# Differential attention on one core: the second map scaled by GpSimd alone, and three of four transposed copies on ScalarE

## What is computed

```python
sc = jnp.einsum('bqhmd,bkhmd->bmhqk', qb, k).astype(jnp.float32) * scale + bias[None, None]
p = jax.nn.softmax(sc, axis=-1)
a = p[:, 0] - lam * p[:, 1]
return jnp.einsum('bhqk,bkhd->bqhd', a.astype(v.dtype), v)
```

## Time and profile before

| what | value |
|---|---|
| median of 3 runs | 4088.17 us (4086.8 to 4090.68) |
| profiled execution, its own time | 4092.34 us |
| profiled execution, its span | 4090.5 us |
| TensorE busy | 3788.4 us (93%) |
| VectorE busy | 2234.5 us (55%) |
| ScalarE busy | 1657.8 us (41%) |
| GpSimd busy | 2488.2 us (61%) |
| differential stage, first maximum to last output | 1177.5 to 1697 us, and once more in the second layer |

### The profile page before, as it was taken

How to read it: one execution, slowest core, us unless ns; L and a number is a source line. 1 busy time by engine, 2 the same in 40 slices (tenths; PEclk the granted TensorE clock), 3 DMA queues, 4 the chain that set the end, 5 groups by cost and what they waited for, 6 DMA issues and landing times. The chain is left out here.

```text
span 4090.5 us, 51527 instructions
## 1 busy us (share of the span) xinstructions
PE 3788.4 (93%) x19002; PEld 2626.4 (64%) x19002; DVE 2234.5 (55%) x3991; ACT 1657.8 (41%) x2882; POOL 2488.2 (61%) x1393
## 2 busy tenths in 40 slices
PE   8999999999989899789889999999999898997898
PEld 8788774555546565558787897755555465655587
DVE  3012135555569999675430021255555699996754
ACT  3112104333358888661031121033333588886610
POOL 1221326877769999755512213277777699997555
PEclk9999999999989999999989999999999899999999
DMA  5333534342220222325353335323322202223353
GB/s 178 124 138 117 169 115 109 78 101 64 57 56 1 56 56 52 91 83 184 130 177 124 129 120 152 130 57 75 75 65 57 56 1 56 56 52 90 88 181 129
DMA packets 179680, 391.38 MB, mean 96 GB/s; under 512 B 17854, under 2 KB 98984, under 8 KB 167784
## 3 DMA queue, kind: packets, MB, share of 16 engines
q1 hardware_dynamic: 178568, 386.70, 33.9%
q10 hardware_dynamic: 864, 1.41, 0.2%
HBM read 254.88 MB, written 135.67 MB: 95 GB/s over the span
## 5 line engine op out<-in xcount | busy, mean ns | idle before, releaser
L1279 POOL TENSOR_TENSOR mla_sum_pool<-mla_sum_pool,mla_probs 128x1024 f32<-128x1024 f32 (+1 forms) x336 | 777.9, 2315 | 207.0 <-ACT mla_probs L1240 182.2
L1297 DVE TENSOR_REDUCE carry_row_max<-psum 128x1 f32<-128x512 f32 x688 | 474.4, 690 | 413.6 <-PE psum L1112 409.1
L1240 ACT ACTIVATE mla_probs<-psum 128x1024 f32<-128x1024 f32 x384 | 373.3, 1021 | 693.6 <-PE psum L1149 686.4
L1545 ACT ACTIVATE diff_probs<-psum,diff_shift 128x1024 f32<-128x1024 f32 x512 | 566.1, 1111 | 195.3 <-DVE diff_shift L1620 189.7
L1613 DVE TENSOR_REDUCE diff_row_max<-psum 128x1 f32<-128x1024 f32 x512 | 612.5, 1218 | 52.5 <-PE psum L1480 38.3
L1492 PE MATMUL psum<-ident,diff_probs 128*128 128x128 f32 x2048 | 329.8, 284 | 107.1 <-DVE diff_turned L1647 72.6
L624 PE MATMUL psum<-in_x_hi,in_w_hi 128*128 128x512 f32 x1024 | 404.5, 395 | 2.7 <-ACT in_mla_val L733 2.7
L624 PE MATMUL psum<-carry_firsts,in_w_hi 128*128 128x512 f32 x1024 | 404.8, 395 | 0.0
L624 PE MATMUL psum<-in_x_hi,in_w_lo 128*128 128x512 f32 x1024 | 401.6, 392 | 0.0
L1492 PEld LDWEIGHTS psum<-ident,diff_probs 128*128 128x128 f32 x2048 | 215.8, 141 | 285.5 <-issue 188.5
L1162 PE MATMUL psum<-mla_probs,mla_v_op 128*64 128x512 f32 x1536 | 373.1, 607 | 0.0
(11 more groups left out here) (206 smaller groups left out, 7369.1 us busy)
## 6 DMA issues: line engine op xcount, KB each, us to landing
in_w_raw<-in_w_in SPq DMA_DIRECT2D x64, 512.0 KB, 3.9
split_d<-in_out SPq DMA_DIRECT2D x64, 512.0 KB, 2.6
raw_d<-in_out SPq DMA_DIRECT2D x32, 512.0 KB, 2.6
mq_d<-in_out SPq DMA_DIRECT2D x48, 256.0 KB, 3.4
mk_d<-in_out SPq DMA_DIRECT2D x48, 256.0 KB, 3.8
carry_firsts<-split_d SPq DMA_DIRECT2D x48, 256.0 KB, 7.9
carry_weights<-split_d SPq DMA_DIRECT2D x48, 256.0 KB, 7.7
carry_weights<-split_d SPq DMA_DIRECT2D x16, 768.0 KB, 17.7
```

The source lines that it names most:

```text
L1240: nc.scalar.activation(probs[:, s % RING, :].rearrange("p (a n) -> p a n", n=CH), psum[:, S0 + 2 * (s % 2):S0 + 2 * (s % 2) + 2, :], ACT.E ...
L1279: nc.gpsimd.tensor_tensor(acc, start, probs[:, s % RING, mine], ALU.add).then_inc(pool_added, 1)
L1297: nc.vector.tensor_reduce(row_max[:, u % 2, qb, n:n + 1], psum[:, sweep_bank(g), :], AX.X, ALU.max).then_inc(maxed, 1)
L1545: nc.scalar.activation(dst[:, half * HALF:(half + 1) * HALF].rearrange("p (a n) -> p a n", n=CH), banks(n, m, half), ACT.Exp, bias=shift[: ...
```

## The change

GpSimd now scales all of `probs1` itself, with a tensor_scalar whose factor is the per-partition number, 1024 keys at a time, each followed by its add. ScalarE no longer scales (L1552 is gone). C0 moves from VectorE to ScalarE, where it stands behind C3 and ahead of E00. On TensorE S01 moves ahead of T3, directly behind S00. The scaling in the windowed attention becomes a tensor_scalar as well.

```diff
@@ tensor program @@
                     if on:
                         scores(n, 0, 0)
+                        scores(n, 0, 1)
                     turns(n - LAG - 1, 3)
-                    if on:
-                        scores(n, 0, 1)
                     products(n, 0)
                     turns(n - LAG, 0)
...
@@ scalar program @@
-                def scale(n):
-                    act.wait_ge(ratio_ready, n + 1)
-                    first = probs1[:, n % DEEP1, 0:CH]
-                    nc.scalar.activation(first, first, ACT.Copy, scale=ratio[:, n % 2:n % 2 + 1]).then_inc(act_scaled, 1)
...
                     copy(n - LAG - 1, 3)
+                    copy(n - LAG, 0)
                     if on:
                         exp(n, 0)
                     copy(n - LAG, 1)
-                    if 1 <= n <= UNITS:
-                        scale(n - 1)
...
@@ gpsimd program @@
-                    second, third = probs1[:, n % DEEP1, CH:HALF], probs1[:, n % DEEP1, HALF:SEQ]
-                    nc.gpsimd.tensor_tensor(second, second, ratio[:, n % 2:n % 2 + 1].broadcast_to([P, HALF - CH]),
-                                            ALU.mult).then_inc(times_ratio, 1)
-                    pool.wait_ge(act_scaled, n + 1)
...
+                    for half in range(2):
+                        at = slice(half * HALF, (half + 1) * HALF)
+                        nc.gpsimd.tensor_scalar(probs1[:, n % DEEP1, at], probs1[:, n % DEEP1, at],
+                                                ratio[:, n % 2:n % 2 + 1], None, ALU.mult).then_inc(times_ratio, 1)
+                        pool.wait_ge(times_ratio, 2 * n + half + 1)
+                        nc.gpsimd.tensor_tensor(probs[:, n % DEEP, at], probs[:, n % DEEP, at],
+                                                probs1[:, n % DEEP1, at], ALU.add).then_inc(mixed, 1)
...
@@ vector program @@
                         to_shift(n, 0)
-                    copy(n - LAG, 0)
                     ratios(n - 1)
...
@@ windowed attention, gpsimd program @@
-                        nc.gpsimd.tensor_tensor(row, row, inv[:, qb % 2, h:h + 1].broadcast_to([P, w]), ALU.mult
+                        nc.gpsimd.tensor_scalar(row, row, inv[:, qb % 2, h:h + 1], None, ALU.mult
                                                 ).then_inc(scaled, 1)
```

More of the change, by code:

```diff
@@ L1405, in diff_attention @@
             sem(n) for n in ("scored", "maxed", "shifted", "exped", "summed", "inverted", "ratio_ready"))
-        act_scaled, times_ratio, mixed, turn_done, copied, pv_done, odd_out, o_ready = (
-            sem(n) for n in ("act_scaled", "times_ratio", "mixed", "turn_done", "copied", "pv_done", "odd_out", "o_ready"))
+        times_ratio, mixed, turn_done, copied, pv_done, odd_out, o_ready = (
+            sem(n) for n in ("times_ratio", "mixed", "turn_done", "copied", "pv_done", "odd_out", "o_ready"))
         def banks(n, m, half):
```

## The result

The changed kernel takes 4439.49 us (median of 4 runs) against 4089.43 us for the kernel before, 1.0853 of its time with a 95% interval of 1.0837 to 1.087. That is 350 us more. I had forecast slower, but with 4161 us and an upper end of 4205: the direction was right and the size was far off.

The account below looks back on a forecast made before the run. GpSimd bounded the kernel at 7.83 us a unit; afterwards a ring through the early C0 would, at 8.47. +78 us for units and -5 for the stage's end gave +73, 4161 us on the median, range 4115 to 4205.

Parts of the forecast that it names:

- I take 1.04 to 1.3 us: Differential stage, GpSimd: assumed time of one tensor_scalar of 1024, giving GpSimd 6.97 us a unit (7.5 at 1.3).
- the tensor_scalar is dear: Rival: at 1.896 us each, GpSimd needs 8.68 us a unit, and the kernel takes 4199 us; chance 0.14.
- GpSimd as the pace: Differential stage: GpSimd, full at 7.83 us a unit before, would stop being the pace and idle about 1 us a unit.
- The end of the stage: Differential stage's end: GpSimd, no longer behind, would finish 2.6 us sooner in each layer, -5 us.
- three signs that I had set for being wrong: ScalarE still waiting for the shift, GpSimd still full, or one spacing for both kinds of block.
- C0 ahead of E00, T3 ahead of T0: Differential stage: E00 waits for C0, hence S01, T3, PV0 and T0: 3.70 us (half 1), 3.35 (half 0).
- The longer ring: Differential stage: loop through the early C0, 8.83 us (half 1), 8.13 (half 0), mean 8.47; +78 us; chance 0.70.
- the old ring: Differential stage: PSUM-slot loop of scores, maxima, shifts and exponentials, 7.74 us a unit (band in half 1), 7.04 (half 0).
- S01 ahead of T3: TensorE: S01 no longer late by T3's wait for VectorE's copy (0.56 us), a gain already counted in the ring.
- The faster rival: C0 is not late, so the loop before the change remains: 7.5 us a unit on the mean, 4043 us; chance 0.08.
- The windowed attention at zero: GpSimd's shorter multiply there is hidden behind other engines: zero; at most 168 x 0.4 us as a gain.
- The clock: Rival: TensorE's clock falls to 1.2 GHz part of the time, lengthening units, above 4210 us; chance 0.04.

Follow-up runs that it names:

- after_no_scale: Changed kernel with GpSimd scaling only 2 columns of each half of the second map, and the windowed attention in its old form: 4166.63 us.
- after_two_ops: Changed kernel with a second operation, an add of zero, in every new tensor_scalar: 4164.28 us.
- after_moves_back: Changed kernel, one-operation tensor_scalar kept, with C0 back on VectorE behind sh0 and S01 back behind T3: 4435.97 us.
- two_ops_c0_only: Changed kernel with add-of-zero tensor_scalars and T3 ahead of S01 again, so only C0's move to ScalarE is kept: 4122.11 us.
- before_two_ops: Kernel before with only GpSimd's two differential-stage multiplies changed, to tensor_scalar with an add of zero: 4077.03 us.
- two_ops_c0_back: Changed kernel with add-of-zero tensor_scalars and both moves undone (C0 on VectorE, S01 behind T3), GpSimd alone scaling: 4074.11 us.
- two_ops_c0_late: Changed kernel with add-of-zero tensor_scalars and C0 on ScalarE but behind the first map's exponentials: 4341.58 us.

## Why the prediction failed

**What failed is one price, "I take 1.04 to 1.3 us" for the tensor_scalar.** It is 2.85 us. I drew it from the rows by the number of tensors read, and that rule did not hold: this form reads one tensor and is slower than the one that reads two. My upper bound, the broadcast multiply at 1.896 us, was not an upper bound. An instruction that a trace does not show need not lie between its neighbours; nothing but the wish for a bound said that it could not be worse than the one that it replaced. The rival "the tensor_scalar is dear" named the right mechanism, with 8.68 us a unit, and had 0.14. With 2.847 its own formula gives 2 x 2.847 + 4.75 + 0.14 = 10.58 us, and the trace has 10.52; 128 x (10.52 - 7.83) is +344 us, and the spans differ by 345. The prediction itself had worked out that the price does not matter below 1.62 us; at 2.85 it is all that matters. So the direction came out right by another mechanism than the forecast one: the loss that I had forecast is real, but the larger one hides it.

**The Trainium skill's rule for one input did not hold for this form.** The Trainium skill, GPSIMD Engine Reference, section 4.1, has operations with one input at about line rate. The copy agrees (1.040 us) and so do the mult and add pairs (1.04 to 1.19 us); the tensor_scalar with one operation does not (2.84), nor the one with max (3.70). The measurement decides.

**GpSimd as the pace: right before on the mean, wrong after.** It is full before and full after. That it would have idle time was wrong. The end of the stage did not get shorter but longer: the last add ends 17.6 us behind the last ratio (1842.85 to 1860.44 in the first layer), where it was 9.6 before. Two of the three signs that I had set for being wrong came: GpSimd full, and one spacing for both kinds of block, 10.51 and 10.53.

**C0 ahead of E00, T3 ahead of T0: right, and hidden.** The longer ring is shown by after_no_scale and after_two_ops, to 0.02 us a unit on the mean and 6 us in all. In the changed kernel GpSimd's 10.52 us cover it: after_moves_back has the same time. The step from the old ring was not right: I had 1.09 us, and in blocks 9 to 13 it is 8.85 - 8.03 = 0.82, since the old ring was longer than summed. On the mean over the blocks this does not show, because GpSimd's 7.83 was taken as the starting point and is right.

**S01 ahead of T3: counted in one place only.** The prediction has T3's 0.56 us in the way through the early copy, and two_ops_c0_only bears that out (4122 against 4164). Of S01's move by itself it named only a gain. With C0 on VectorE the move costs some 41 to 44 us, by way of VectorE's order.

**The faster rival.** It needed C0 not to be late. C0 was late wherever both moves were kept; with the form out of the way, E00 started 1.04 us behind its shift (after_no_scale).

**The old ring and its distance from GpSimd's pace.** I summed 7.74 us with 1.26 from an exponential to its scores, a spacing read in one place. Over blocks 9 to 13 the spacing of E00 is 8.03 us, in the kernel before too, and one unit of them shows the 0.27 more. GpSimd's own spacing is 7.81 to 7.89 us throughout the second head, and the E00 swing around it, 7.64 and 8.03, since the rings of `probs` let GpSimd lag. In the long blocks it catches up, in the short ones it falls behind. So in these blocks the ring stood above GpSimd's pace and not 0.1 us below it, and taking GpSimd out as the pace gave 13 to 16 us (before_two_ops, two_ops_c0_back) and not the 45 to 54 that I then expected.

**The windowed attention at zero.** It was to be hidden either way, and I only thought of a gain. GpSimd is now without idle time there (L1807), and the second layer's end came 3.6 us later, the first's not. That is 1% of the loss.

**The clock** had no visible part in the changed kernel's loss. It is 1.00 from 1425 to 1550 us in both kernels, with TensorE busy 70% of it after. Over the whole stage in the first layer it is 0.96 after (1178 to 1866 us) and 0.98 before (1178 to 1697 us), and still every unit of the second head takes 10.51 to 10.53 us. In two_ops_c0_late the clock did cost time.

## What to carry to other kernels

Before an instruction form goes into a loop that an engine paces, time that form alone, on that engine, with its operations and operands as they will be. A bound read from neighbouring rows is a guess as soon as the row itself is missing. On an engine that is full, an error of 0.95 us in each of 256 instructions makes 244 of the 255 us that the form cost against the broadcast one.

When a copy or any other step is put ahead of another on an engine that works in order, add up the way to that step's own input. If that is longer than what the step behind it waits for, the difference is paid in every turn of the ring; if it is not put ahead, look who else waits behind it. A change can hold two losses of which the larger hides the smaller, so undo each with the other gone: mending the form alone leaves 4164 us, undoing the moves alone 4436, both together 4074.

## What the runs showed of the hardware that I had not expected

GpSimd's tensor_scalar on float32 with one operation, mult or add, takes 2842 ns for 1024 columns and 1562 for 512, that is 2.5 ns a column; with a constant in place of the per-partition number 2767. With a second operation that changes nothing, an add of zero or a mult by one, it takes some 1120 ns, with two constants 1044, about the copy's 1040. With add and max it takes 3699. The broadcast tensor_tensor, 1892, lies between. The simplest way to write a multiply by a number is not the fastest, and in this kernel the add of zero is worth 275 us.

In two_ops_c0_late TensorE's granted clock was 0.84 or 0.85 in six of 16 blocks, and those were the six long ones: there the clock was paid for in the spacing of the units. In the changed kernel, where GpSimd sets the pace, it was not.
